# Hybrid pooling/S5 backbone layer on one core: conditioning products in four column tiles, tables moved behind the tiles, and tiles turned by diagonal products

## What is computed

```python
def _layer(x, cvec, p, rows, h0):
    sh1, sc1, g1, sh2, sc2, g2 = split(silu(cvec) @ w_ada + b_ada, 6)
    h = rmsnorm(x, norm_mix) * (1 + sc1) + sh1
    proj = h @ w_in
    pool_out = pool_mixer(proj[..., :512], ...)        # mean windows, linear map, scale
    ssm_out, finals = ssm_mixer(proj[..., 512:], h0)   # complex diagonal scan both ways, GELU, GLU
    x = x + g1 * (concat(pool_out, ssm_out) @ w_out)
    h = rmsnorm(x, norm_mlp) * (1 + sc2) + sh2
    return x + g2 * (square(relu(h @ w_mlp1)) @ w_mlp2), finals
```

## Time and profile before

| | |
|---|---|
| median of 3 runs | 1266.99 us (1266.74 to 1267.92) |
| the profiled execution's own time | 1267.88 us |
| its span on the core | 1266.0 us |
| PE, PE weight load, DVE, ACT, POOL busy | 1172.5, 1024.1, 844.3, 334.3, 474.6 us |
| HBM read, written | 89.86 MB, 9.49 MB |
| share of the chain that ended last | PE 72%, DVE 21%, issue 2%, ACT 2% |

### The profile page before, as it was taken

The page is one execution under the profiler, slowest core; times in us unless marked ns, Lnnn a source line. Parts: engine busy times, 40 slices in busy tenths (PEclk is TensorE's granted clock), DMA queues, the critical chain, the costliest instruction groups (busy, mean ns, idle before and its releaser), DMA issues.

```text
span 1266.0 us, 18412 instructions
## 1 busy us (share of the span) xinstructions
PE 1172.5 (93%) x6417; PEld 1024.1 (81%) x6417; DVE 844.3 (67%) x1315; ACT 334.3 (26%) x621; POOL 474.6 (37%) x418
## 2 busy tenths in 40 slices
PE   6799997725899999999999999999999999999997
PEld 0389994414787888989989989899899899898896
DVE  5995999999795677456465564564564654645648
ACT  4464225323334673101102112011011021120114
POOL 2702102401000533472562652743724626527430
PEclk9889999767899999999999999999999999999999
DMA  9615425963512232011021120120110210211003
GB/s 325 206 40 131 101 101 194 258 168 98 167 36 84 83 117 68 16 52 50 17 66 33 33 66 33 33 66 17 50 50 16 66 37 30 66 33 33 33 1 150
DMA packets 61556, 102.00 MB, mean 81 GB/s; under 512 B 9518, under 2 KB 43374, under 8 KB 61260
## 3 DMA queue, kind: packets, MB, share of 16 engines
q1 hardware_dynamic: 54312, 78.79, 20.0%
q0 software_dynamic: 5680, 19.11, 4.9%
q10 hardware_dynamic: 1524, 3.56, 0.9%
HBM read 89.86 MB, written 9.49 MB: 78 GB/s over the span
## 4 chain that ended last, share of the span: by engine, by line
PE 72%; DVE 21%; issue 2%; ACT 2%; DMA 1%; ACTq 1%; DVEq 0%
PE bank L1427 23%; PE bank L1429 23%; PE bank L1428 23%; DVE fold_p L1127 2%; DVE fold_q L1125 2%; DVE fold_q L1126 2%; PE bank L1436 2%; DMA raw<-in_w_ada 1%; DVE sums L1228 1%; DVE states_b L1133 1%; DVE states_b L1130 1%; DVE fold_pq L1016 1%; PE bank L1463 1%; DVE acc L1411 1%; DVE x_lo L1040 1%
## 5 line engine op out<-in xcount | busy, mean ns | idle before, releaser
L559 POOL TENSOR_TENSOR acc<-acc,gated 128x512 f32<-128x512 f32 x270 | 373.1, 1382 | 375.8 <-DVE gated L1363 339.2
L1427 PE MATMUL bank<-x_hi,w_hi 128*128 128x384 f32 x960 | 323.6, 337 | 4.5 <-issue 3.1
L1429 PE MATMUL bank<-x_hi,w_lo 128*128 128x384 f32 x960 | 321.7, 335 | 0.0
L1428 PE MATMUL bank<-x_lo,w_hi 128*128 128x384 f32 x960 | 321.6, 335 | 0.0
L1363 DVE TENSOR_TENSOR gated<-bank,gate_b 128x512 f32<-128x512 f32 x270 | 182.6, 688 | 115.5 <-PE bank L1429 99.3
L1427 PE MATMUL bank<-w_hi,f_hi 128*128 128x512 f32 x576 | 224.2, 389 | 1.2 <-DVE w_lo L1344 1.2
L1429 PE MATMUL bank<-w_hi,f_lo 128*128 128x512 f32 x576 | 224.4, 390 | 0.0
L1428 PE MATMUL bank<-w_lo,f_hi 128*128 128x512 f32 x576 | 224.3, 389 | 0.0
L906 ACT ACTIVATE relu<-bank 128x384 f32<-128x384 f32 x96 | 47.2, 493 | 649.3 <-PE bank L1429 646.3
L1353 DVE TENSOR_TENSOR f_tmp<-relu 128x384 f32<-128x384 f32 x96 | 64.7, 674 | 205.6 <-ACT relu L906 205.6
L1427 PEld LDWEIGHTS bank<-x_hi,w_hi 128*128 128x128 f32 x960 | 180.9, 188 | 8.2 <-issue 6.5
(11 more groups left out here) (297 smaller groups left out, 1336.9 us busy)
## 6 DMA issues: line engine op xcount, KB each, us to landing
raw<-in_w_mlp SPq DMA_DIRECT2D x64, 512.0 KB
raw<-in_w_ada SPq DMA_DIRECT2D x48, 512.0 KB
out<-acc SPq DMA_DIRECT2D x9, 512.0 KB, 2.6
x_tile<-in_x_sample POOLq DMA_DIRECT2D x8, 512.0 KB, 8.6
raw<-in_w_in SPq DMA_DIRECT2D x8, 512.0 KB
raw<-in_w_out SPq DMA_DIRECT2D x8, 512.0 KB
x_again<-in_x_sample POOLq DMA_DIRECT2D x8, 512.0 KB, 3.7
u_rows<-proj ACTq DMA_DIRECT2D x4, 576.0 KB, 3.3
```

What stands on the lines that cost most here:

```text
L559: GP.tensor_tensor(a, a, BT[i % 4][:], ALU.add).then_inc(s.acc, 1)
L1427: mm(out, sh_, mh, start=first, stop=False)
L1428: mm(out, sh_, ml, start=False, stop=False)
L1429: return mm(out, sl, mh, start=False, stop=last)
```

## The change

Parts of it:
- `ada_unit` makes four products of 256 columns, each into its own 32-row strip of one bank (four column tiles), where two products of 512 columns were. The bias is done in the same way.
- The rows are copied in halves of 256 (`first_row`) to two buffers. The two rows of the first part are copied after the root of tile 5 and turned before PE's last unit; the second part's follow behind the bias (`first_turn`).
- `root_diag` scales the 128x128 identity by the inverse roots of tile t. `turn_scaled` multiplies each block of the raw x tile by that diagonal, an fp32 product with the x block as the stationary side; the in-place scaling of the tiles is gone.
- Of the tables, 0 stays ahead of the tiles and one operation of table 1 within; the rest are built behind the tiles. Tables 2 to 5 come before the scan, with weight 2's split ahead of table 4, and tables 6 and 7 after step 1.
- `STATES_AT`, `WB_AT`, `SPLIT_AT` and `BESIDE` have other numbers.

```diff
--- before.py
+++ after.py
@@ -35,16 +35,16 @@
 GB = G // 2
 MAP_AT = (6, 10)
 C_AT = (13, 17)
-STATES_AT = (5, 7)
+STATES_AT = (6, 8)
 ADA_AT = {14: 0, 16: 1, 18: 2, 21: 3, 22: 4, 23: 5}
-SPLIT_AT = (2, 8, 14, 19)
+SPLIT_AT = (2, 5, 9, 14)
 FINAL_ORDER = (0, 1, 2, 3, 8, 4, 5, 6, 7)
-WB_AT = {2: (0, 1), 3: (4, 5), 4: (2, 3), 5: (6, 7), 23: tuple(range(8, 16))}
+WB_AT = {3: (0, 1), 4: (2, 3), 5: (4, 5, 6, 7), 23: tuple(range(8, 16))}
 WB_ORDER = [k for a in sorted(WB_AT) for k in WB_AT[a]]
 TABLES = [(0, 0, 0), (0, 0, 1), (0, 1, 0), (0, 1, 1), (1, 1, 0), (1, 1, 1), (1, 0, 0), (1, 0, 1)]
 IN_SEQ = [(0, 0), (1, 0), (0, 1), (0, 2), (1, 1), (1, 2)] + [(i, g) for i in range(2, 8) for g in range(NG)]
 IN_END = {i: a for a, (i, g) in enumerate(IN_SEQ)}
-BESIDE = {4: (0, 0, 3), 5: (0, 3, 6), 6: (0, 6, 8), 7: (1, 0, 3), 8: (1, 3, 8)}
+BESIDE = {5: (0, 0, 3), 6: (0, 3, 6), 7: (0, 6, 8), 8: (1, 0, 8)}
 
 KBYTE = 1024
 RESERVED = 16 * KBYTE + 128
@@ -70,10 +70,11 @@
 
     XS = [at(f"x_tile{i}", [P, D], R_W + 4 * i * KBYTE if i < 6 else R_A + 4 * (i - 1) * KBYTE) for i in range(TT)]
     SQ0 = at("square_dump0", [P, D], R_A + 16 * KBYTE)
+    RD0 = at("root_diag", [P, TT, P], R_W + 24 * KBYTE)
     TPB = at("table_tmp", [P, D], R_A + 16 * KBYTE)
     HT0 = [at(f"h_tile{i}", [P, KB, P], o) for i, o in enumerate((R_S, R_P, R_P + 10 * KBYTE))]
     BIAS0 = at("ada_bias0", [1, 2048], R_P)
-    ROW0 = at("ada_row0", [2, 512], R_P + 8 * KBYTE)
+    ROW0 = [at("ada_row0", [2, 512], R_P + 8 * KBYTE), at("ada_row1", [2, 512], R_X)]
     BX = at("b_re_im", [P, Q, SP], R_P + 10 * KBYTE)
     BY = at("b_im_re", [P, Q, SP], R_P + 14 * KBYTE)
     small = [R_U]
@@ -628,18 +629,23 @@
             S.activation(w_split_bufs(w)[0][:], RAW[n % 4][:], ACT.Copy).then_inc(s.w_hi, 1)
 
         act.wait_ge(s.tabs, 2)
+        def first_row(part, hf):
+            n = 2 * part + hf
+            act.wait_ge(s.ada_mm, part + 1)
+            if n >= 2:
+                act.wait_ge(s.ada_cols, n - 1)
+            for i in range(2):
+                j = 2 * hf + i
+                S.activation(ROW0[hf][:, 256 * i:256 * i + 256], BANK[part][32 * j:32 * j + 2, 0:256], ACT.Copy).then_inc(s.row_ready, 1)
+
         for t in range(TT):
             act.wait_ge(x_in[t], 16)
             stats(t, XS[t][:], SQ0[:], 0)
-
-        n_row = 0
-        for part in range(2):
-            for hf in range(2):
-                act.wait_ge(s.ada_mm, part + 1)
-                if n_row:
-                    act.wait_ge(s.ada_cols, n_row)
-                S.activation(ROW0[:], BANK[2 * part + hf][0:2, :], ACT.Copy).then_inc(s.row_ready, 1)
-                n_row += 1
+            if t == 5:
+                for hf in range(2):
+                    first_row(0, hf)
+        for hf in range(2):
+            first_row(1, hf)
         act.wait_ge(s.ada0, 2)
         act.wait_ge(s.tabs, 3)
         affine(0, HT0, 0, 0)
@@ -1020,10 +1026,12 @@
             tt(out, out, tmp, ALU.add).then_inc(s.ca_ready, 1)
             dve.wait_ge(s.ca_ready, 4 * b + 2 * d + h + 1)
 
-        def normed(t, src, dst, base):
-            dve.wait_ge(s.root, base + t + 1)
+        def root_diag(t):
+            dve.wait_ge(s.root, t + 1)
+            if t == 0:
+                dve.wait_ge(s.id_ready, 1)
             then(V.reciprocal(STAT[2][:, t:t + 1], STAT[1][:, t:t + 1]))
-            ts(dst, src, STAT[2][:, t:t + 1], None, ALU.mult).then_inc(s.xn, 1)
+            ts(RD0[:, t, :], ID[:], STAT[2][:, t:t + 1], None, ALU.mult).then_inc(s.xn, 1)
 
         def affine(t, ht, ada, base):
             cond = 0 if t < L else 1
@@ -1085,14 +1093,12 @@
         tt(BY[:], BY[:], TB[:], ALU.add).then_inc(s.tabs, 1)
         dve.wait_ge(s.tabs, 3)
 
-        to_state(0, TPQ)
-        to_state(1, TPQ)
         for t in range(TT):
-            normed(t, XS[t][:], XS[t][:], 0)
-        to_state(2, TPQ)
-        dve.wait_ge(s.ada_cols, 4)
+            root_diag(t)
+        to_state(0, TPB)
         for k in range(4):
-            cols = BANK[7][:, 64 + 8 * k:72 + 8 * k].rearrange("p (k a) -> p a k", a=2)
+            dve.wait_ge(s.ada_cols, 2 + 2 * (k // 2))
+            cols = BANK[6 + k // 2][:, 64 + 8 * k:72 + 8 * k].rearrange("p (k a) -> p a k", a=2)
             if k < 2:
                 ada_scale(ADA[0], cols, 16, k)
             else:
@@ -1103,14 +1109,10 @@
             if t + 1 < TT:
                 affine(t + 1, HT0, 0, 0)
             if t == 0:
-                to_state(3, TPB, (0,))
-            if t == 4:
-                to_state(4, TPB, (0,))
+                to_state(1, TPB, (0,))
             round_lo(t, HT0, 0)
             if t < 2:
                 split_lo(t, FIRST_IN + t)
-            if t == 3:
-                to_state(3, TPB, (1, 2))
         def fold(b, level, q0, nq, src, dst):
 
             nr, nk = src.shape[2], src.shape[3]
@@ -1247,14 +1249,17 @@
 
 
         dve.wait_ge(s.h_lo, TT)
-        to_state(4, TPB, (1, 2))
+        to_state(1, TPB, (1, 2))
+        for n in range(2, 4):
+            to_state(n, TPB)
+        split_lo(2, FIRST_IN + 2)
+        to_state(4, TPB)
         to_state(5, TPB)
-        to_state(6, TPB)
-        split_lo(2, FIRST_IN + 2)
         def beside_first(k):
             if k == 1:
+                split_lo(3, FIRST_IN + 3)
+                to_state(6, TPB)
                 to_state(7, TPB)
-                split_lo(3, FIRST_IN + 3)
             if k in SPLIT_AT:
                 w = 4 + SPLIT_AT.index(k)
                 split_lo(w, FIRST_IN + w)
@@ -1428,30 +1433,47 @@
             mm(out, sh_, ml, start=False, stop=False)
             return mm(out, sl, mh, start=False, stop=last)
 
-        def ada_unit(n, banks, k):
-
+        def ada_unit(part, k):
+            n = part * KB + k
             raw_landed(pe, n)
             cv = COL[:, 0:16].rearrange("p (a k) -> p a k", a=2)[:, :, k]
-            for hf in range(2):
-                last = mm(BANK[banks[hf]][0:2, :], cv, RAW[n % 4][:, hf * 512:hf * 512 + 512], start=(k == 0), stop=False)
+            for j in range(4):
+                last = mm(BANK[part][32 * j:32 * j + 2, 0:256], cv, RAW[n % 4][:, 256 * j:256 * j + 256], start=(k == 0), stop=False,
+                          skip_group_check=True)
             last.then_inc(s.ada_used, 1)
+
+        def first_turn(n):
+            pe.wait_ge(s.row_ready, 2 * (n + 1))
+            for i in range(4):
+                last = PE.transpose(BANK[6 + n // 2][:, 64 + 8 * n + 2 * i:66 + 8 * n + 2 * i], ROW0[n % 2][:, i * P:(i + 1) * P], ID[0:2, 0:2])
+            last.then_inc(s.ada_cols, 1)
 
         pe.wait_ge(s.silu_done, 1)
         for part in range(2):
             for k in range(KB):
-                ada_unit(part * KB + k, (2 * part, 2 * part + 1), k)
+                ada_unit(part, k)
+                if part == 1 and k == KB - 2:
+                    pe.wait_ge(s.id_ready, 1)
+                    for n in range(2):
+                        first_turn(n)
             pe.wait_ge(s.bias0_in, 32)
             pe.wait_ge(s.sgn_ready, 3)
-            for hf in range(2):
-                last = mm(BANK[2 * part + hf][0:2, :], ONE[:], BIAS0[:, part * D + hf * 512:part * D + hf * 512 + 512],
-                          start=False, stop=True)
+            for j in range(4):
+                last = mm(BANK[part][32 * j:32 * j + 2, 0:256], ONE[:], BIAS0[:, part * D + 256 * j:part * D + 256 * j + 256],
+                          start=False, stop=True, skip_group_check=True)
             last.then_inc(s.ada_mm, 1)
-        pe.wait_ge(s.id_ready, 1)
-        for k in range(4):
-            pe.wait_ge(s.row_ready, k + 1)
-            for i in range(4):
-                last = PE.transpose(BANK[7][:, 64 + 8 * k + 2 * i:66 + 8 * k + 2 * i], ROW0[:, i * P:(i + 1) * P], ID[0:2, 0:2])
-            last.then_inc(s.ada_cols, 1)
+        for n in range(2, 4):
+            first_turn(n)
+
+        def turn_scaled(t):
+            pe.wait_ge(s.xn, t + 1)
+            if t >= 2:
+                pe.wait_ge(s.aff_d, 4 * (t - 1))
+                pe.wait_ge(s.aff_a, 4 * (t - 1))
+            for k in range(KB):
+                last = mm(turn_banks(t)[k // 4][:, (k % 4) * P:(k % 4 + 1) * P], XS[t][:, k * P:(k + 1) * P], RD0[:, t, :],
+                          start=True, stop=True, skip_group_check=True)
+            last.then_inc(s.tr, 1)
 
         def turn_tile(t, src, base):
 
@@ -1473,7 +1495,7 @@
                 if a >= 4:
                     pe.wait_ge(s.in_ev, a - 3)
                 else:
-                    pe.wait_ge(s.row_ready, a + 1)
+                    pe.wait_ge(s.row_ready, 8)
             wh = WH[i % 2][:].rearrange("p (k f) -> p k f", k=KB)
             wl = WL[i % 2][:].rearrange("p (k f) -> p k f", k=KB)
             for k in range(k0, k1):
@@ -1485,7 +1507,7 @@
         for t in range(TT):
             if t == 1:
                 pe.wait_ge(s.ada0, 2)
-            turn_tile(t, XS[t], 0)
+            turn_scaled(t)
             if t in BESIDE:
```

## The result

The changed kernel takes 1271.97 us (median of 6 runs, 1271.10 to 1273.92) where the kernel before, in runs beside it, takes 1267.75 us (6 runs). The ratio is 1.0034, with a 95% interval of 1.0023 to 1.0045: **slower by 4.2 us**. The forecast was 1266.0, its range ended at 1270.0, and slower had a chance of 0.12.

What follows compares the result with a forecast made beforehand. The prediction took PE and what feeds it to be the limit ahead of 106 us, then DVE's scan. Its terms, -6.6 + 3.5 + 2.1 = -1.0 us, gave 1266.0 us against a median of 1266.99, range 1262.2 to 1270.0.

Steps and rivals of the forecast that it cites:

- The last piece lands at 39.8: Conditioning: the last w_ada load lands at 39.8 us, from 41.5 with full queues and 2 us got back; bounds 39.3 and 42.3.
- Unit, bias, copies: 3.8 us: Behind the last load: one unit 0.9, bias 0.9, two copies with turns 2.0 us, so tiles start at 43.6.
- Turning tiles 0 and 1: PE turns the first two x tiles from a cold clock in 6.2 us, bounds 5.3 and 7.0.
- Tile 1 to E: From DVE's scale and shift of tile 1 to block 3's end: 9.6 + 24.0 + 0.8 us.
- E: Mark where PE's block 3 ends; forecast at 84.2 us instead of 90.82, 6.6 us earlier.
- E to the first states: PE from block 3's end to the first state products: 16.0 us instead of 12.5, 3.5 us later.
- The waits: DVE's scan waits for high halves of late weights: 1.3 us at weight 5, 1.5 at weight 7.
- Part three: DVE from first states to scan step 14: 3.7 - 4.4 + 1.3 + 1.5, 2.1 us more.
- A shift at step 14 arrives whole: DVE does not stand still for 165 us after scan step 14, so a shift there reaches 324 us whole.
- The clock rule: PE's clock rose with only transposes running, so the kind of product was costed at nothing for the clock.
- the fourth: Conditioning loads: no gain from the DMA, last piece lands at 42, +1 us, 1268.0 us; chance 0.14.
- The fifth: PE's clock stays low in the tiles, 6.0 us instead of 0.8, +4.2, 1271.2 us; chance 0.13.

Runs made afterwards that it cites:

- e9: Changed kernel with the four b table loads issued behind ACT's second x tile, near 22 us, instead of at 5 to 7 us; 1270.91 us, one execution.
- e1: Changed kernel with the two groups of state products back behind blocks 5 and 7 (STATES_AT alone undone); 1272.40 us, 1.0047 of the kernel before.
- e5: Changed kernel with the low halves of weights 5, 6 and 7 split behind scan steps 8, 14 and 19 again (SPLIT_AT alone undone); 1268.65 us.
- e2: Changed kernel with tiles scaled in place on DVE and turned as plain transposes, the diagonal products alone undone; 1267.88 us, 1.0002 of the kernel before.
- e7: Changed kernel with plain transposes of tiles scaled on DVE, and old places of states (STATES_AT) and splits (SPLIT_AT); 1262.65 us, 0.9966 of the kernel before.
- e11: e7 with x tiles 4 to 8 loaded later, tiles 7 and 8 scaled behind DVE's tiles 4 and 5; 1263.74 us, 0.9971 of the kernel before.
- e3: Changed kernel with conditioning units as two products of 512 columns again (column tiling alone undone); 1272.71 us, 1.0044 of the kernel before.
- e4: Changed kernel plus 66 identity products, results unread, in the gaps between conditioning units; 1272.13 us, 1.0036 of the kernel before.
- e8: Changed kernel with loads of x tiles 4 to 8 held back to conditioning units 5, 7, 9, 14 and 16; 1270.98 us, 1.0035 of the kernel before.

## Why the prediction was wrong, point by point

- **"The last piece lands at 39.8": this step failed.** It landed at 43.93, outside its bounds of 39.3 and 42.3, and 0.96 us later than in the kernel before (42.97). Two things were wrong in it. First, "213 GB/s, since the ring was held by PE's first units": the row had a DMA share of 1.04 beside its 213 GB/s, so the engines were busy, and e9 shows with what. Freed buffers brought no byte sooner (12.78 MB by 38 us, 12.89 before). The 2 us to be got back did not exist, and the end would have been 41.5 (less 2 that is 39.5, so 39.8 has a slip of 0.3 in it). Second, "3.5 us at 414 GB/s" took the last piece to be in when all bytes are. 14.27 of the 14.3 MB were in at 42.0, but in 42 to 44 us only 17 packets of 2 KB and more are left, the end of `w_ada`, beside 879 smaller ones, nearly all of `w_in`, whose loads SP issues from 41.20 on. So it landed 2.4 us behind 41.5. Two loads of `w_in` were issued in 42 to 44 us, and one in the kernel before; that they hold up the last packets fits the later landing, and no run tests it. The kernel before's own landing, 42.97, would have spoken against 41.5.
- *"Unit, bias, copies: 3.8 us"* was 4.8: the turns of part 0 stood ahead of the last unit (it could have started at 43.9 and started at 44.53), and the copies took 0.4 more. So the tiles started 5.1 us late, 4.1 for the landing and 1.0 for this.
- *Turning tiles 0 and 1* took 5.9 us from the start of the tiles to DVE's tile 1; I had 6.2. *Tile 1 to E* took 33.67; I had 34.4. Both right, and so is the low clock that I took for the units. With the start at 48.74 the sum gives E 89.3, 1.0 from the truth.
- *E to the first states* 16.06 us; I had 16.0. *The waits* 1.98 and 1.48; I had 1.3 and 1.5. *Part three* +2.37; I had +2.1. Right in size. What I did not draw from them: with waits behind it that end on PE, the 3.5 us of the states' place and the waits of the weights are not two costs to be undone one by one. e1 and e5 show it, 0 and 3.3 us alone, 6.0 together.
- *A shift at step 14 arrives whole*: M moved by 3.37 us and the span by 3.4. Right for these two traces; in five of the experiments' a copy that meets POOL's memset behind the scan adds 1.0 to 1.8 us.
- *The clock rule.* I costed the kind of product at nothing for the clock. In e2, with transposes only from 48.54, a tile takes 1.06 us at 53.91, after 4.85 us for the three before, so the clock rose without ordinary products; the changed kernel's products need 9.56 us for four tiles (5.9 of it up to DVE's tile 1) and bring no earlier rise. The rule of the Trainium skill (TensorE: Matmul & The Clock Gate, Part 4: PE-mode transpose) is not borne out for the rise. Later, with gaps between tiles, tiles 4 and 5 are turned in 1.94 us each in e7 and e11, and the products of the changed kernel take 2.02 us each there, their length at the higher clock. That would fit the rule as well as it fits mere amount of work; no run here parts the two.
- *The rivals.* The nearest was the fourth, no gain from the DMA, +1 us: its mechanism is the right one, and its size was off, since I let the last piece be in at 42. The fifth would have given 1271.2, close to the time, for another reason: the clock did not fall in the tiles (PE's products at 60.85 and 64.40 us ran at the higher one).

## What to carry to other kernels

A low transfer rate with a DMA share near 1 is not room to be had: ask which packets are under way. And where a stage hangs on one piece, take from the trace when that piece landed, and not when all bytes would be in at a rate of another stretch. Two delays in series in front of one consumer can cover each other, so undo them together as well as singly before one is called free. And where an engine is made faster than its loads, count what its idle time does to its clock: here 1.6 us gained in the units were 1.9 us lost in the turns right behind them (e3).

## What the runs showed of the hardware that was not expected

- 1.0 MB of b tables, in packets of 4 KB to 64 partitions, holds all queues at a share of 1.03 and 200 to 300 GB/s in all for as long as it is under way, whenever it is issued (e9: 410 GB/s at 12 to 16 us, 297 and 303 at 22 to 26).
- The granted clock of the profile can be wrong for a long stretch. In e5 it is 1.00 from 14 to 54 us and units take 1.03 us as in the changed kernel, where it is 0.50. e4's units at the higher clock take 0.61. The length of a known instruction is the better witness.
- Four executions of one program up to E differ by 1.1 us there (87.92 to 89.03), with 64 records in 9.56 to 10.50 us: the moment at which the clock rises is not the same each time. E of single profiles is no finer than this.
- Five short copies of DVE between the scans (0.18 to 0.22 us each, at 253 to 266 us) lie close to a memset of POOL of 1.97 us that PE releases. In e2, e3, e4, e5 and e9 a copy starts within it and ends 0.03 to 0.07 us behind its end, after 1.17 to 1.99 us; in the nine other traces the copies are done by its start, and none is long. DVE's sums and products of the scan run beside the memset at their usual length (0.27 us at 263.54 in the changed kernel, memset from 263.26 to 265.23). Which of the two comes first changes M by up to 1.8 us, and a small shift decides it, so a gain at E can shrink on its way to M (4.2 to 2.9 us in e2). No run moves the memset to test it.

Not tried: e8's gates with the last x tile sooner, or ACT's share of tile 0 ahead of the last statistics. By e8 and e11 the tiles would then start 2.4 to 2.75 us sooner without the wait on ACT.
